# Half of the unsplit tiles split again, and expert weights in rows of 8 KB

## The reference, cut to what matters

```python
D_MODEL = 1024; SEQ = 256
N_EXPERTS = 8; TOP_K = 2; EXPERT_FF = 3584

def swiglu_2(x, w_gate, w_up, w_down):
    return (jax.nn.silu(x @ w_gate) * (x @ w_up)) @ w_down

def moe_ffn(h, router_w, router_b, w_gate, w_up, w_down):
    b, s, d = h.shape
    t = h.reshape(b * s, d)
    logits = (t @ router_w).astype(jnp.float32) + router_b.astype(jnp.float32)
    top_vals, top_idx = lax.top_k(logits, TOP_K)
    top_w = jax.nn.softmax(top_vals, axis=-1)
    gates = jnp.sum(jax.nn.one_hot(top_idx, N_EXPERTS, dtype=jnp.float32) * top_w[..., None], axis=1)
    out = jnp.zeros((b * s, d), jnp.float32)
    for e in range(N_EXPERTS):
        y = swiglu_2(t, w_gate[e], w_up[e], w_down[e]).astype(jnp.float32)
        out = out + gates[:, e:e + 1] * y
    return out.astype(h.dtype).reshape(b, s, d)
```

## Time and profile before

| | us |
|---|---|
| three runs | 2607.22, 2611.96, 2613.63 |
| median | 2611.96 |
| the profiled execution | 2611.29 |
| its span | 2609.4 |
| TensorE, VectorE, ScalarE busy in the span | 2528.4, 1971.3, 1457.1 |

### The profile page before, as it was taken

One profiled execution on the slowest core, in us unless ns is written; L12 is line 12 of the kernel. 1 busy time (PEld: TensorE's weight loads), 2 busy tenths in 40 slices (PEclk: granted clock), 3 DMA queues, 4 the chain that ended last, 5 costly groups with the idle time before them and its releaser, 6 DMA issues.

```text
span 2609.4 us, 45404 instructions
## 1 busy us (share of the span) xinstructions
PE 2528.4 (97%) x17582; PEld 2116.0 (81%) x17601; DVE 1971.3 (76%) x1938; ACT 1457.1 (56%) x1511; POOL 88.3 (3%) x82
## 2 busy tenths in 40 slices
PE   8999999999999999999999999999999999999998
PEld 7888888888888888888888989787678678767765
DVE  6666886667666886667666774789888989889897
ACT  5444423445444423445544662577777876877686
POOL 6000005000000000000000000000000000000000
PEclk9999999999999999999999999899999999999999
DMA  8555313555556312655556530799999999999995
GB/s 281 193 184 178 120 51 96 188 186 181 188 186 191 120 51 82 193 192 178 176 190 178 150 127 3 276 362 360 394 388 354 381 393 381 355 394 392 346 370 209
DMA packets 342893, 601.45 MB, mean 230 GB/s; under 512 B 11984, under 2 KB 180816, under 8 KB 342608
## 3 DMA queue, kind: packets, MB, share of 16 engines
q1 hardware_dynamic: 335264, 590.85, 65.2%
q10 hardware_dynamic: 7472, 8.35, 1.0%
HBM read 598.11 MB, written 1.05 MB: 230 GB/s over the span
## 4 chain that ended last, share of the span: by engine, by line
PE 49%; DMA 28%; DVE 12%; DVEq 5%; ACT 4%; issue 2%; ACTq 0%; another core or an unknown queue 0%; SPq 0%; PEld 0%; PEldq 0%
DMA raw<-in_ffn_w_down 13%; PE ps L3023 7%; DVE wlo L317 7%; PE ps L568 6%; DMA raw<-in_w_in 6%; PE ps L3028 4%; PE ps L592 4%; DVEq L319 4%; DMA raw<-in_moe_w_gate 4%; PE ps L3071 4%; PE ps L571 3%; ACT whi L312 3%; PE ps L3076 2%; PE ps L857 2%; PE ps L3008 2%
## 5 line engine op out<-in xcount | busy, mean ns | idle before, releaser
L317 DVE TENSOR_TENSOR wlo<-raw,whi 128x2048 fp32r<-128x2048 f32 x382 | 875.2, 2291 | 176.7 <-ACT whi L312 166.4
L312 ACT CAST whi<-raw 128x2048 fp32r<-128x2048 f32 x382 | 727.2, 1909 | 373.1 <-DMA raw<-in_ffn_w_down 142.7
L568 PE MATMUL ps<-xboth,whi 128*128 128x512 f32 x1680 | 420.8, 392 | 0.0
L568 PEld LDWEIGHTS ps<-xboth,whi 128*128 128x128 f32 x1680 | 305.3, 189 | 57.2
L3023 PE MATMUL ps<-whi,xboth 128*128 128x512 f32 x1248 | 329.1, 400 | 6.3 <-issue 5.0
L3023 PEld LDWEIGHTS ps<-whi,xboth 128*128 128x128 f32 x1248 | 230.2, 190 | 56.4 <-issue 9.7
L317 DVE TENSOR_TENSOR wlo<-U,whi 128x2048 fp32r<-128x2048 f32 x100 | 229.0, 2290 | 24.7 <-ACT whi L312 16.9
L571 PEld LDWEIGHTS ps<-xboth,wlo 128*128 128x128 f32 x1680 | 229.2, 190 | 16.4
L571 PE MATMUL ps<-xboth,wlo 128*128 128x256 f32 x1680 | 234.2, 282 | 0.0
L3028 PE MATMUL ps<-wlo,xboth 128*128 128x512 f32 x800 | 219.4, 396 | 9.4 <-DVE wlo L317 8.7
L312 ACT CAST whi<-U 128x2048 fp32r<-128x2048 f32 x100 | 190.6, 1912 | 48.0 <-DMA U<-in_moe_w_up 33.8
(11 more groups left out here) (591 smaller groups left out, 3784.9 us busy)
## 6 DMA issues: line engine op xcount, KB each, us to landing
raw<-in_moe_w_gate SPq DMA_DIRECT2D x58, 1024.0 KB, 9.9
raw<-in_moe_w_up SPq DMA_DIRECT2D x56, 1024.0 KB, 7.7
U<-in_moe_w_up SPq DMA_DIRECT2D x56, 1024.0 KB, 8.9
U<-in_moe_w_down SPq DMA_DIRECT2D x56, 1024.0 KB, 9.5
raw<-in_ffn_w_gate SPq DMA_DIRECT2D x55, 1024.0 KB, 5.3
raw<-in_ffn_w_up SPq DMA_DIRECT2D x55, 1024.0 KB, 5.4
raw<-in_ffn_w_down SPq DMA_DIRECT2D x55, 1024.0 KB, 5.0
work<-in_moe_w_gate SPq DMA_DIRECT2D x54, 1024.0 KB, 9.8
```

The costliest lines, as they stand in the source:

```text
L312: act.copy(whi[:, n % SPLIT if place is None else place, 0:width], buf[:, 0:width]).then_inc(hi_ready[n % RAW], 1)
L317: dve.tensor_tensor(wlo[:, at, 0:width], buf[:, 0:width], whi[:, at, 0:width], ALU.subtract).then_inc(split_ready[at], 1)
L568: pe.matmul(ps[:, first_bank + b, :], whi[:, n % SPLIT, c * GW + b * P:c * GW + (b + 1) * P], xboth[:, c].rearrange("p a t -> p (a t)"), s ...
```

## The change

The list of unsplit tiles loses every second entry: groups 1, 3 and 5 of a small item keep theirs, and groups 2, 4 and 6 split that tile as the others are split. The host lays the three expert weights out anew, tile after tile, each as 128 rows of 2048 floats; a tile is then loaded with one run of 8 KB for each partition. What lies where in a landed tile is as before, and so is the number and size of the transfers. The host's work is not part of the device time.

```diff
+def expert_tiles(w, down):
+
+    w = np.asarray(w).reshape((E, EF // 512, 2, 2, P, D) if down else (E, 2, C // 2, P, EF // 512, 512))
+    w = w.transpose((0, 1, 2, 4, 3, 5) if down else (0, 4, 1, 3, 2, 5))
+    return np.ascontiguousarray(w).reshape(-1, TILE)
...
+        def load_whole(sp, n, src, slot_of):
+            buf, landed, free_ = slot_of(n)
+            take(sp, free_)
+            sp.dma_start(buf, src).then_inc(landed, 16)
...
-        WHOLE = [ITEM_TILES + 6 * g + 3 for g in range(EN - 1)]
+        WHOLE = [ITEM_TILES + 6 * g + 3 for g in range(0, EN - 1, 2)]
...
-            def in_half(m, w, e, g, k):
-                load_tile(sp, m, cols(w, e * D + k * HALF, g * EW, EW, C // 2), slot_of)
-
-            def down_half(m, e, g, k):
-                load_tile(sp, m, cols(wd, e * EF + g * EW + k * GW, 0, D, 2), slot_of)
+            def half(m, w, e, g, k):
+                load_whole(sp, m, w[bass.ds(e * (2 * EN * P) + (2 * g + k) * P, P), :], slot_of)
...
-                        down_half(m + i, e, g - 1, k)
+                        half(m + i, wd, e, g - 1, k)
...
-                        in_half(m + i, wg if i % 6 < 2 else wu, *((e, g) if g < EN else (nxt, 0)), k)
+                        half(m + i, wg if i % 6 < 2 else wu, *((e, g) if g < EN else (nxt, 0)), k)
...
-        v = np.ascontiguousarray(inputs[name])
+        if name in ("moe_w_gate_2", "moe_w_up_2", "moe_w_down_2"):
+            v = expert_tiles(inputs[name], name == "moe_w_down_2")
+        else:
+            v = np.ascontiguousarray(inputs[name])
```

More of the change, by code:

```diff
@@ L2938, in moe_stream @@
         def moe_stream(sp, n, l):
-            wg, wu, wd = (a[k].rearrange("o e r c -> (o e r) c") for k in ("moe_w_gate_2", "moe_w_up_2",
-                                                                          "moe_w_down_2"))
+            wg, wu, wd = (a[k] for k in ("moe_w_gate_2", "moe_w_up_2", "moe_w_down_2"))
             def expert(i):
@@ L2957, in tiles @@
                     if i % 6 >= 4:
-                        down_half(m + i, e, g - 1, k)
+                        half(m + i, wd, e, g - 1, k)
                     else:
-                        in_half(m + i, wg if i % 6 < 2 else wu, *((e, g) if g < EN else (nxt, 0)), k)
+                        half(m + i, wg if i % 6 < 2 else wu, *((e, g) if g < EN else (nxt, 0)), k)
             for k in range(2):
-                in_half(n + k, wg, 0, 0, k)
+                half(n + k, wg, 0, 0, k)
             for k in range(2):
-                in_half(n + 2 + k, wu, 0, 0, k)
+                half(n + 2 + k, wu, 0, 0, k)
             n += 4
@@ L2982, in moe_stream @@
             for k in range(2):
-                down_half(n + 2 * ITEM_TILES - 6 + k, e1, EN - 1, k)
+                half(n + 2 * ITEM_TILES - 6 + k, wd, e1, EN - 1, k)
             return n
```

## The result

The changed kernel takes 2622.9 us, the median of 6 runs (2619.4 to 2627.1); the kernel before takes 2612.3 (2607.2 to 2614.2) on the same chip. The ratio is 1.0045, 95% interval 1.0035 to 1.0055: slower by 10.6 us (forecast: 12.8), and over the 0.3% that the prediction calls a difference. The profiled execution of the changed kernel is the fastest of its six, 2619.4 us, so a difference of two profiles shows some 2.5 us too little.

What follows compares the result with a forecast made beforehand. The prediction took VectorE to set the pace in the small item: 3.2 us later in each of four, 12.8 us, with ScalarE, SP and layout at 0. 2611.3 + 12.8 gave 2624 us, range 2605 to 2635.

Steps and rivals of the forecast that it cites:

- VectorE sets the pace in the small item, and its slack is used up: Small item: VectorE gains 7.3 us of splits against 3.1 us of slack, so its waits fall from 4.1 to below 1.5.
- ScalarE: ... Cost nothing.: Small item: ScalarE gains 5.7 us of copies but has 24 us free of 111, so no cost.
- D = 3.2: TensorE's lateness against before at a small item's end, 3.2 us, taken for four items as 12.8 us.
- the steps: TensorE's lateness through a small item: 2.4 us after groups 2 and 3, 2.7 after 4 and 5, 3.2 after 6.
- the lead: VectorE's work ahead of TensorE in a small item, said to cover 1.0 us of the added time.
- Layout ... I take 0: Expert-stage weight transfers: 8 KB rows move faster, but nobody waits for a landing, so worth 0 us.
- rival 5: 8 KB rows move badly or instruction packets queue behind them, each such stop doubled costing 5 to 10 us; chance 0.03.
- The packet's cost: Expert-weight DMA: 18 ns fixed plus 0.0354 ns a byte, so 308 ns for an 8 KB packet.
- The large item keeps its length.: Large items of the expert stage: their length was to stay as before the change.
- rival 2: Split buffers store large-item slack and absorb the added splits: 2611 to 2615 us, no difference; chance 0.20.
- Rival 1: TensorE is the bound and VectorE's splits fit in, giving 20.9 us back: 2590 us; chance 0.10.
- rival 4: None of VectorE's added splits is absorbed: 29.2 us slower, 2640 us; chance 0.10.

Runs made afterwards that it cites:

- experiment 5: Changed kernel, but VectorE subtracts only 64 of the 2048 columns of the 12 newly split tiles: 2617.3 us, 1.0020 of the kernel before.
- experiment 7: Changed kernel, with only 64 of 2048 columns of the 12 newly split tiles both copied and subtracted: 2615.1 us, 1.0012 of the kernel before.
- experiment 6: Changed kernel, but ScalarE copies only 64 of 2048 columns of the 12 newly split tiles: 2622.2 us, 1.0037 of the kernel before.
- experiment 10: New layout with all six tiles unsplit, loading only the first 4 KB of each expert-tile row: 2607.0 us, 0.9981 of the kernel before.
- experiment 4: Changed kernel with no unsplit tile at all in the small items: 2651.8 us, 1.0154 of the kernel before.
- experiment 8: Changed kernel, with VectorE's carry work in group 2 of small items moved behind that group's last splits: 2624.4 us, 1.0047 of the kernel before.
- experiment 9: New layout with all six tiles unsplit, each contiguous tile moved as 512 rows of 2 KB: 2611.9 us, 1.0000 of the kernel before.
- experiment 1: Changed kernel with all six tiles unsplit again, so the new layout alone: 2606.1 us, 0.9985 of the kernel before.

## Why the prediction came out right, and what in it was wrong

- **VectorE sets the pace in the small item, and its slack is used up.** Right. Its waits went from 4.1 to 0.7 us (forecast: below 1.5), TensorE waits for `wlo` instead, and the item takes 111.7 us (forecast: about 111). But VectorE's seconds are not the whole of the price: with the added subtractions and copies gone, 2.3 of 3.8 us stay (experiments 5 and 7). That part has no term in the sum; experiment 7 argues that it is VectorE's order and the reach of three buffers. L3016 has the 96 records for `raw` and none for `U`:

```profile
L3016 PE MATMUL ps<-raw,work x96: 592/592/644, 1806.0 to 2576.2; 128*64 128x512 f32 x96
```

- **"ScalarE: ... Cost nothing."** Right for its time (experiment 6), but its copy is 1.91 of the 4.2 us that a refill takes (experiment 7).
- **"D = 3.2", the same in four pairs: the mis-sized term.** Within an item the steps were met. By the turns of the loop's three small items, TensorE is late by 1.8 to 3.0 us after group 2, 2.4 to 2.6 after groups 3 and 4, 2.6 to 2.9 after group 5 and 3.0 to 3.2 after group 6 (forecast: 2.4, 2.4, 2.7, 2.7, 3.2). Behind that come 0.6 us more where the next large item begins (15.7 to 16.3 us from the third item's last turn), which the steps leave out. So an item costs 3.8, the full 7.3 less 3.1 of slack and less 0.4 for the lead that I had put at 1.0. The last item cost 7.8. From 2500 us on VectorE had less slack before than in the third item (1.7 us of waits for copies, against 4.1), and there is no gather behind it to lengthen TensorE's groups. That isn't all of it: experiments 5 and 7 gave back only 1.6 and 1.8 of the 6.1 us by which TensorE is late at the item's last turn. Marks of that turn, behind group 6, and a low product after it, before and after:

```profile
2590.33 0.46 PE L3058 MATMUL ps<-con,work 64*128 64x64 f32 x4
...
2593.03 1.09 PE L3076 MATMUL ps<-wlo,hhi 128*128 128x512 f32 x4
```
```profile
2596.93 0.46 PE L3066 MATMUL ps<-con,work 64*128 64x64 f32 x4 [1.88 <-DVE work L3294]
...
2599.78 1.91 PE L3084 MATMUL ps<-wlo,hhi 128*128 128x512 f32 x4
```

  From 2519.85 (before) and 2520.32 (after), the turns of the item's group 2, 70.5 us became 76.6: TensorE was late by 6.1 at the last turn, and 1.6 more after it. I had taken the third item for all four. Sum: 3 x 3.8 + 7.8 = 19.2 by the traces; by the medians the splits cost 17.2, or 15.3 with long rows, against 12.8.
- **"Layout ... I take 0": the other mis-sized term.** It is -4.7 us by the medians. The reason for 0, that nobody waits for a landing, holds (experiment 10). What it missed is VectorE's stop for `issue` after the loop. The prediction did name this stop, in rival 5, with the wrong sign: it became shorter with longer rows. That instruction packets queue behind data, as the rival has it, no run shows. Time to landing fell, as forecast: median 6.8 us from 9.1, longest 10.7 from 15.7.
- **The packet's cost.** I solved 308 ns for 8 KB from two stretches. The stretch of the earlier trace rows in the changed kernel:

```profile
q1 hardware_dynamic: 24711, 180.01, 95.5%
```

  95.5% of 16 x 480 us over 24711 packets is 297 ns for 7285 B: by such means 5% less for a byte than before (101.8 ns for 2372 B), not 12%. But these stretches mix packets, some 2700 of 4 B and 9 ns in each among them. Sorted by length in the traces from 1940 to 2420 us, data packets take, median and mean, 86 and 89 ns for 2 KB and 161 and 169 for 4 KB before, and 309 and 333 for 8 KB after. So the 308 ns were right for the median packet, and a byte costs 7% less by the means and 10% by the medians. That lies between the 12% of my mix and the 3%, an estimate worked out from the Trainium skill, page "DMA: Bandwidth & Descriptors", section "Bandwidth" (Why small descriptors are slow). The forecast of some 45 thousand packets in the stage was met, with 47869.
- **"The large item keeps its length."** Right for the middle ones, 122.0 us by the turns before and after, so nothing is absorbed there (rival 2). Wrong for the fourth: 123.9 us with the splits alone, for 127.6 before. There 3.7 us come back, with a stop of 3.1 us for 5.4; without this piece of luck the forecast of 12.8 would have been further off.
- **Rival 1** was tried from the other side by experiment 4 and falls; **rival 4** (29.2 us) overstates: 15 to 17.

The forecast of 2624 against 2623 is thus better than its working. That it is so near is luck: two errors of 2.5 to 4.7 us nearly cancel. Its mechanism, VectorE's pace, is right in kind and covers 1.5 of the 3.8 us of a small item by the runs.

**The version to keep** is the layout with all six tiles unsplit, 2606.1 us: 0.9985 (0.9976 to 0.9994) of the kernel before and some 15 us under the changed one.

## What to carry to other kernels

Giving an engine more work costs what exceeds its slack, but here taking the work away again refunded less than half of it. The added tiles also moved the other splits in VectorE's order, behind its carry work, and shortened the cover between freeing a buffer and needing it filled. So write down that order and work out that distance in microseconds, beside the engines' totals. Add up a periodic schedule item by item, and treat the last item, which has nothing behind it, by itself. When two parts of a change are forecast, run each alone: the total here agreed to 2 us while one part was off by 4.7 and the other by up to 4.4. And compare several items before a wait is given a price: the third item alone would have made the half clock a cost.

## What the runs showed of the hardware

- After a stand of TensorE of 1.8 to 2.0 us the granted clock may fall or not. In the changed kernel there are four such stands in the second down tile of group 2, one for each small item. After the one that ended at 2298.65 the granted clock from 2299 to 2303 us was 0.57 of 2.4 GHz in the mean, so mostly 1.2 GHz, and four matmuls took 1.73 us. After the other three, the one of 1829.20 among them, they took 1.19. After the stands of 2.6 to 2.7 us in experiment 8 the four products took 2.07 us in all four items, and the granted clock from 2303 to 2307 us was 0.57. What it costs depends on who sets the pace: groups 2 and 3 took 32.2 us with and without the half clock.
- VectorE's stop after the loop's end is shorter beside rows of 8 KB, 2.8 and 2.9 us for 5.4, 5.4 and 5.6 beside rows of 2 and 4 KB, though no data transfer is waited for; with half the bytes it is 4.8. TensorE stands 0.8 to 0.9 us at the loop's return in some passes and 2.0 to 2.8 in others, with either layout. That instruction transfers are served sooner between fewer and longer packets would explain the first, but is not shown.
- Row lengths of 2 and 8 KB move 380 GB/s alike (experiments 9 and 1, 1940 to 2420 us); with the longer ones the data packets' time is a smaller share of that of the 16 engines:

```profile
DMA packets 25050, 182.60 MB, mean 380 GB/s; under 512 B 2781, under 2 KB 2781, under 8 KB 2781
...
q1 hardware_dynamic: 25028, 182.26, 96.6%
```
```profile
q1 hardware_dynamic: 91659, 182.04, 103.3%
```
